# Expert blocks run in pairs, with rows turned two blocks ahead, and one dt product over 32 columns

## What is computed

```python
def expert_block(args):
    xb, e = args
    hb = jax.nn.silu(xb @ w_gate[e]) * (xb @ w_up[e])     # 2048 -> 512
    return hb @ w_down[e]                                 # 512 -> 2048
...
dt = jax.nn.softplus(dt_raw + dt_bias)      # dt_raw = the last 16 columns of h @ w_in
```

## Time and profile before

| | us |
|---|---|
| median of 3 runs | 2782.51 (2777.09 to 2786.82) |
| the profiled execution's own time | 2786.49 |
| its span, first to last instruction | 2784.8 |
| mean granted TensorE clock | 0.96 |

### The profile page before, as it was taken

How to read it: one execution, slowest core, us unless ns; L and a number is a source line. 1 busy time by engine, 2 the same in 40 slices (tenths; PEclk the granted TensorE clock), 3 DMA queues, 4 the chain that set the end, 5 groups by cost and what they waited for, 6 DMA issues and landing times.

```text
span 2784.8 us, 30586 instructions
## 1 busy us (share of the span) xinstructions
PE 2555.2 (92%) x11884; PEld 1529.8 (55%) x11884; DVE 1304.6 (47%) x1520; ACT 604.5 (22%) x859; POOL 296.9 (11%) x498
## 2 busy tenths in 40 slices
PE   4999999999999787899999499999999898999894
PEld 3577888888768666678887233333333333333331
DVE  4379999999766667544324411211122111111114
ACT  4122222222212365332344100000000000000003
POOL 0000000000111011010000011111111111111112
PEclk8999999999999879999999699999999999999997
DMA  9833333333676632655543999999949999799986
GB/s 337 314 115 99 98 106 98 98 109 107 215 225 202 223 122 87 253 171 155 199 161 131 401 408 417 353 401 407 410 143 383 410 408 362 278 415 401 413 325 254
DMA packets 233453, 710.94 MB, mean 255 GB/s; under 512 B 26266, under 2 KB 120618, under 8 KB 184790
## 3 DMA queue, kind: packets, MB, share of 16 engines
q1 hardware_dynamic: 186624, 555.56, 51.8%
q0 software_dynamic: 36736, 123.18, 14.4%
q10 hardware_dynamic: 9996, 30.86, 2.9%
HBM read 657.60 MB, written 70.86 MB: 262 GB/s over the span
## 4 chain that ended last, share of the span: by engine, by line
PE 37%; DMA 19%; DVE 2%; issue 0%; ACT 0%; POOL 0%; SPq 0%; ACTq 0%; DVEq 0%; POOLq 0%
PE ps L1696 15%; DMA ring<-in_w_up_dram 9%; DMA ring<-in_w_down_dram 9%; PE ps L1710 7%; PE ps L1916 4%; PE ps L1918 4%; PE ps L1917 4%; PE ps L1719 1%; PE ps L1636 1%; DVE tmp L2162 0%; PE ps L1931 0%; PE ps L1728 0%; DMA xrow<-h_d,tix 0%; DVE hidT L2455 0%; PE ps L1661 0%
## 5 line engine op out<-in xcount | busy, mean ns | idle before, releaser
L1696 PE MATMUL ps<-ring,xT 128*64 128x512 f32 x3136 | 702.2, 605 | 40.9 <-DMA ring<-in_w_up_dram 39.5
L1696 PEld LDWEIGHTS ps<-ring,xT 128*64 128x64 f32 x3136 | 232.5, 140 | 502.6 <-issue 499.0
L1710 PE MATMUL ps<-ring,hidT 128*64 128x512 f32 x1568 | 348.6, 596 | 10.8 <-DVE hidT L2455 6.0
L744 PE MATMUL ps<-hh,wih 128*128 128x512 f32 x1056 | 330.6, 394 | 7.4 <-DVE wil L732 7.4
L2450 DVE TENSOR_TENSOR hb<-ps,gsl 128x256 f32<-128x256 f32 x49 | 20.8, 424 | 673.5 <-ACT gsl L2125 673.5
L744 PE MATMUL ps<-hh,wil 128*128 128x512 f32 x1056 | 330.8, 394 | 0.0
L744 PE MATMUL ps<-hl,wih 128*128 128x512 f32 x1056 | 329.7, 393 | 0.0
L1115 DVE SCALAR_TENSOR_TENSOR acc<-u,vcur,acc 128x1024 f32<-128x1024 f32 x240 | 308.2, 1284 | 7.8
L2125 ACT ACTIVATE gsl<-ps 128x256 f32<-128x256 f32 x49 | 18.8, 383 | 1080.9 <-PE ps L1696 1080.9
L744 PEld LDWEIGHTS ps<-hh,wih 128*128 128x128 f32 x1056 | 198.7, 189 | 55.6 <-DVE wil L732 8.2
L1710 PEld LDWEIGHTS ps<-ring,hidT 128*64 128x64 f32 x1568 | 107.7, 137 | 217.9 <-issue 190.9
(11 more groups left out here) (387 smaller groups left out, 2907.8 us busy)
## 6 DMA issues: line engine op xcount, KB each, us to landing
ring<-in_w_gate_dram SPq DMA_DIRECT2D x128, 1024.0 KB, 30.1
ring<-in_w_up_dram SPq DMA_DIRECT2D x128, 1024.0 KB, 31.9
ring<-in_w_down_dram SPq DMA_DIRECT2D x64, 2048.0 KB
wm<-in_w_mod_dram POOLq DMA_DIRECT2D x88, 512.0 KB, 4.2
wraw_i<-in_w_in_dram SPq DMA_DIRECT2D x72, 512.0 KB, 3.9
wraw_o<-in_w_out_dram SPq DMA_DIRECT2D x128, 256.0 KB, 3.3
wmA<-in_w_mod_dram SPq DMA_DIRECT2D x32, 512.0 KB, 8.2
u<-in_w_mod_dram POOLq DMA_DIRECT2D x24, 512.0 KB, 4.6
```

What stands on the lines that cost most here:

```text
L744: last = pe.matmul(ps[:, 1024 * r + 512 * h:1024 * r + 512 * h + 512], w[:, s, k, :], x_[:, t, 512 * h:512 * h + 512], start=(t == 0 and n ...
L1696: last = pe.matmul(ps[BLK * a:BLK * a + BLK, BANK_GU:BANK_GU + FE], xT[:, t, h, :], ring[:, s:s + 2, c0:c0 + FE // 2], start=(q + k == 0), ...
L1710: last = pe.matmul(ps[BLK * a:BLK * a + BLK, BANK_D + 512 * n:BANK_D + 512 * n + 512], hidT[:, t, h, :], ring[:, slot(o, 8 + d), c0:c0 + 512],
```

## The change

In the first 29 experts (`PHASED`) the blocks of an expert are taken in passes of at most two; with an odd count the first pass has one block. A pass runs `gate_up`, all eight row turns (now of the block after the next) and `transpose_hidden` for each of its blocks, and then `down` for each. TensorE, VectorE and GpSimd each run nested loops for this: over passes, and in each pass over blocks, twice. The bounds are computed in registers (`passes`, `pass_blocks`). The turned hidden rows are kept in `hidR`, and copied from there in four parts of 64 columns into `hidT`. `down` makes one half of the output columns with all four parts and then the other; slots are released in the second. The output rows are scaled in two halves. The rows' scaling and shift are done in four quarters of 256 columns, each once `gate_up` has read that quarter of `xT`, and ahead of the hidden product. Gathers run three blocks ahead of the first in a pass instead of two, and rows of block 1 are turned before the first `gate_up`. In a pass GpSimd issues all gathers and then all scatters. The last three experts keep one block at a time, with the new waits and halves. `dt_proj` has both rounded parts of the weights side by side (32 columns) and two products instead of three; the two halves of the result are summed by a matmul with `dfold`.

```diff
--- before.py
+++ after.py
-NI = MAX_ITEMS + 3
+NI = MAX_ITEMS + 4
+AHEAD = 2
+PHASED = E - 3
...
-                                for n, (w, x_) in enumerate(((wdh, hh), (wdl, hh), (wdh, hl))):
-                                    last = pe.matmul(ps[0:H, 3072 + 512 * h:3584 + 512 * h], w[:, t, :],
+                                for n, x_ in enumerate((hh, hl)):
+                                    last = pe.matmul(ps[0:2 * H, 3072 + 512 * h:3584 + 512 * h], wd[:, t, :],
                                                      x_[:, t, 512 * h:512 * h + 512], start=(t == 0 and n == 0),
-                                                     stop=(t == KT - 1 and n == 2))
+                                                     stop=(t == KT - 1 and n == 1))
...
-                            last = pe.transpose(ps[:, 3584 + j * H:3584 + (j + 1) * H], sq[0:H, j * P:(j + 1) * P], ident[0:H, 0:H])
+                            last = pe.matmul(ps[:, 3584 + j * H:3584 + (j + 1) * H], sq[0:2 * H, j * P:(j + 1) * P], dfold[0:2 * H, :],
+                                             start=True, stop=True)
...
+            def passes(eng, begin, end):
+                count = eng.snap(nc.s_assert_within(end - begin, 1, SEQ // BLK, skip_runtime_bounds_check_because=COUNTED))
+                n = nc.s_assert_within(((count + 1) & 31) >> 1, 1, SEQ // BLK // AHEAD, skip_runtime_bounds_check_because=COUNTED)
+                head = nc.s_assert_within(((count - 1) & (AHEAD - 1)) + 1, 1, AHEAD, skip_runtime_bounds_check_because=COUNTED)
+                return eng.snap(n), eng.snap(head)
+            def pass_blocks(eng, begin, head, p):
+                later = (p + 7) >> 3
+                j0 = begin + (((p + 7) & 7) * AHEAD + head) * later
+                j1 = begin + head + p * AHEAD
+                return tuple(eng.snap(nc.s_assert_within(v, lo, MAX_ITEMS - 1 + lo, skip_runtime_bounds_check_because=COUNTED))
+                             for lo, v in enumerate((j0, j1)))
...
+                    pe.wait_ge(s_hb, j + 1)
                     for q in range(4):
-                        if q % 2 == 0:
-                            pe.wait_ge(s_xT, 2 * j + q // 2 + 1)
+                        pe.wait_ge(s_xT, 4 * j + q + 1)
                         for kind in (GATE, UP):
                             pe.wait_ge(s_we[2 * q + kind], 16 * o + 16)
                         s = slot(o, 2 * q)
                                                  ring[:, s:s + 2, c0:c0 + FE // 2], start=(q + k == 0), stop=(q + k == 6))
                         last.then_inc(s_guq[q], 1)
-                def down(pe, j, o):
-                    for d in range(FT):
-                        h, t = d // 2, d % 2
-                        if h == 0:
-                            pe.wait_ge(s_hT, 2 * j + t + 1)
-                        if t == 0:
-                            pe.wait_ge(s_we[8 + d], 16 * o + 16)
-                        for n in range(2):
+                def down(pe, j, o, turned):
+                    for n in range(2):
+                        pe.wait_ge(s_or, 2 * j + n + 1)
+                        for d in range(FT):
+                            h, t = d // 2, d % 2
+                            if n == 0:
+                                pe.wait_ge(s_hT, 4 * (j + turned) + d + 2)
+                                if t == 0:
+                                    pe.wait_ge(s_we[8 + d], 16 * o + 16)
                             for a in range(2):
                                 c0 = HALF_ROW * a + 512 * n
                                 last = pe.matmul(ps[BLK * a:BLK * a + BLK, BANK_D + 512 * n:BANK_D + 512 * n + 512],
                                                  hidT[:, t, h, :], ring[:, slot(o, 8 + d), c0:c0 + 512],
                                                  start=(d == 0), stop=(d == FT - 1))
-                        last.then_inc(s_dt[d], 1)
-
-                def transpose_rows(pe, ts):
+                            if n == 1:
+                                last.then_inc(s_dt[d], 1)
+                            elif d == FT - 1:
+                                last.then_inc(s_dn, 1)
+                def transpose_rows(pe, j, ts):
                     v = xrow[:].rearrange("p (c t) -> p t c", t=KT // 2)
                     for t in ts:
+                        if t == 0:
+                            pe.wait_ge(s_xr2, 16 * j + 16)
+                        if t % 4 == 0 and not (isinstance(j, int) and j == 0):
+                            pe.wait_ge(s_xm, 4 * j - 2 + t // 2)
                         last = pe.transpose(ps[:, BANK_X + t * P:BANK_X + (t + 1) * P], v[:, t, :], ident[:])
                         if t % 4 == 3:
                             last.then_inc(s_xt2, 1)
                 def transpose_hidden(pe, j):
-                    pe.wait_ge(s_hb, j + 1)
+                    pe.wait_ge(s_hb, j + 2)
                     v = hb[:].rearrange("p (c t) -> p t c", t=2)
                     for t in range(2):
-                        pe.transpose(ps[:, BANK_H + 512 * t:BANK_H + 512 * t + P], v[:, t, :], ident[:]).then_inc(s_hbt, 1)
+                        last = pe.transpose(ps[:, BANK_H + t * P:BANK_H + (t + 1) * P], v[:, t, :], ident[:])
+                    last.then_inc(s_hbt, 1)
...
-                        pool.wait_ge(s_xt2, 2 * i + 4)
-                        gather(i + 2, gix[:, ds(i + 2, 1)])
+                    words, begin = [packed_word(pool, 0)], 0
...
+                        with pool.Fori(0, count) as p:
+                            j0, j1 = pass_blocks(pool, begin, head, p)
+                            with pool.Fori(j0, j1) as i:
+                                pool.wait_ge(s_xt2, 2 * i + 6)
+                                gather(i + 3, gix[:, ds(i + 3, 1)])
+                            with pool.Fori(j0, j1) as i:
+                                scatter(i)
+                        begin = end
+                    with pool.Fori(begin, n) as i:
+                        pool.wait_ge(s_xt2, 2 * i + 6)
+                        gather(i + 3, gix[:, ds(i + 3, 1)])
                         scatter(i)
...
-                    transpose_rows(pe, range(8))
-                    begin = 0
+                    transpose_rows(pe, 0, range(8))
+                    transpose_rows(pe, 1, range(8))
+                    begin, turned = 0, 0
                     for o in range(E):
                         if o % PACK == PACK - 2 and o + 2 < E:
                             words.append(packed_word(pe, o // PACK + 1))
-                        end = blocks_through(words, o)
-                        with pe.Fori(0, end - begin) as b:
-                            j = begin + b
-                            gate_up(pe, j, o)
-                            pe.wait_ge(s_xr2, 16 * j + 32)
-                            transpose_rows(pe, range(7))
-                            transpose_hidden(pe, j)
-                            transpose_rows(pe, range(7, 8))
-                            down(pe, j, o)
+                        end = through(pe, words, o)
+                        if o < PHASED:
+                            n, head = passes(pe, begin, end)
+                            with pe.Fori(0, n) as p:
+                                j0, j1 = pass_blocks(pe, begin, head, p)
+                                done = pe.snap(turned + p)
+                                with pe.Fori(j0, j1) as j:
+                                    gate_up(pe, j, o)
+                                    transpose_rows(pe, j + 2, range(8))
+                                    transpose_hidden(pe, j)
+                                with pe.Fori(j0, j1) as j:
+                                    down(pe, j, o, done)
+                            turned = pe.snap(nc.s_assert_within(turned + n, 1, MAX_ITEMS, skip_runtime_bounds_check_because=COUNTED))
+                        else:
+                            with pe.Fori(begin, end) as j:
+                                gate_up(pe, j, o)
+                                transpose_rows(pe, j + 2, range(7))
+                                transpose_hidden(pe, j)
+                                transpose_rows(pe, j + 2, range(7, 8))
+                                down(pe, j, o, turned)
                         begin = end
...
+                        for q in range(4):
+                            h, a = q % 2, q // 2
+                            v = xT[:, 4 * a:4 * a + 4, h, :]
                             dve.wait_ge(s_xt2, 2 * j + a + 1)
-                            dve.tensor_tensor(xT[:, 4 * a:4 * a + 4, :, :],
-                                              ps[:, BANK_X + 512 * a:BANK_X + 512 * a + 512].rearrange("p (t h r) -> p t h r", t=4, h=2),
-                                              mods(mod_scale, a), ALU.mult).then_inc(s_xm, 1)
-                        for a in range(2):
-                            dve.wait_ge(s_xm, 2 * j + a + 1)
-                            v = xT[:, 4 * a:4 * a + 4, :, :]
```

(72 more changed lines are left out.)

52 lines of the change are left out of this document (36 added, 16 removed).

## The result

The changed kernel takes 3166.26 us (median; 3163.39 to 3169.0) against 2782.96 us for the kernel before on the same chip: ratio 1.1375, 95% interval 1.1356 to 1.1393. Forecast were 2796.5 us and a range of 2772 to 2832. The direction was right, the size was not: +383 us where +14 were expected. The profiled execution has a span of 3161.7 us (2784.8 before).

What follows compares the result with a forecast made beforehand. The prediction took TensorE's work and waits for weights, with clock lost behind them, as alternating limits in the expert stage. Stage +21.0 us, with dt +14.0, on a median of 2782.51 gave 2796.5 us, range 2772 to 2832.

Steps and rivals of the forecast that it cites:

- sequencers exposed: Rival: register arithmetic is not covered, 0.8 us a single pass, words 2.2, pairs 2; 2830 us, chance 0.15.
- Pass end: From gate/up's end to down: longer VectorE chain and copies start down at T + 3.2, +1.4 us each, 33 times.
- Between two gate/ups: Inside a pair, the loop jump and register instructions delay the next gate/up: +0.6 us, 10 times.
- VectorE behind a pair: The second block's output half waits for the first block's scatter, delaying VectorE's next work: +1.0 us, 10 times.
- Packed words: TensorE's load of a word loses the lead of queued down work that hid it: +1.2 us, 7 times.
- Start: Rows of block 1 must be gathered and turned before the first gate/up: +9.6 us, once.
- dt: In the dt products, 32 fewer matmuls save 7.4 us and eight folds cost 0.4: -7.0 us.
- The ring: Weight loads after a full ring issue 27.4 us before the expert ends, not 18.9; DMA runs 8.5 us further ahead.
- segments 1 and 2: Expert-stage blocks 23 to 34 and 35 to 45, each after a full ring; forecast -7.3 and -8.5 us.
- The ring wins: Rival: the longer chain at pass ends is hidden, so only the later start is paid; 2757 us, chance 0.14.
- Clock: Rival: about 1.6 us of TensorE idle at each pass end slows the next quarter; 2851 us, chance 0.06.
- Jumps: Rival: VectorE's nested loops make instructions be fetched again at pass ends, +55 us; 2838 us, chance 0.04.

Runs made afterwards that it cites:

- e6: The changed kernel with the growing sum worked out once a pass into a register, ahead of gate/up, except in the last three experts; 3074.47 us.
- e1: The changed kernel with the number of passes done kept in one TensorE register, one addition a pass, instead of the growing sum; 2804.88 us, ratio 1.0078.
- e5: The changed kernel with a pass-count register, hidden product ahead of the last quarter's scale and shift, hidden turns between row turns 0-3 and 4-7; 2796.22 us.
- e2: The kernel before with only the dt part of the change (two products over 32 columns and the fold); 2779.34 us, ratio 0.9988.
- e8: The changed kernel with a pass-count register, no hidR copy in the chain, part copies reading PSUM, order scale, product, shift; 2783.3 us, ratio 1.0003.
- e4: The kernel before, with blocks and order unchanged, plus the growing sum in an always-met wait ahead of down's matmuls; 3144.28 us, ratio 1.1301.
- e7: The changed kernel with a pass-count register, but down's first wait uses the growing sum except in the last three experts; 3084.4 us, ratio 1.1069.

## Why the prediction was wrong, and where it was right

**The step that failed** is the term "the pass arithmetic is some thirty instructions (about 3 us)", with "The arithmetic alone I cost at nothing, because the lead covers it just about". Three things in it were off. The number wasn't constant: ahead of a down it is 4 instructions in the first pass and 113 in a late one. The place wasn't the head of the pass but down's first wait, behind the hidden turn, where nothing is queued (a gap of 13.67 us for 14.0 us of arithmetic), and each down of a pair pays anew. And even at the head the cover is 3.5 us (e6). In place of nothing the sum cost 361 us (e1). The rate was well taken: 0.1 assumed, 0.12 measured. The rival *sequencers exposed* named this mechanism and gave it 0.15 and 2830: but its price was 0.8 us a single pass, where the late gaps are above 10. Of the 361 us, 304 are those gaps and 72 the matmuls that run slower behind them, less 15 us of waits for weights that vanished.

**Stage, without the sum.** e1 lets the other terms be read. From the first row turn to the end of the last down e1 takes 22.3 us more than the kernel before (1574.50 to 2770.1, against 1574.75 to 2748.1); the sum said +21.0. With dt the forecast was +14, and e1's ratio means +21.7 (14.2 to 29.5). But the parts balance by luck, for some were too dear and one too hopeful:

- *Pass end, +1.4 each.* Measured +1.32 (period 23.85 in e1); down starts 3.1 us after gate/up, forecast T + 3.2, and VectorE's part copy releases it, as said. e5 shows an error inside the chain: the product waits for ScalarE's silu until T + 0.5, and the scale ahead of it is free.
- *Between two gate/ups, +0.6.* +0.45 (16.05 in e1), 0.25 of it "issue".
- *VectorE behind a pair, +1.0.* Nothing. The scatter went as forecast: issued at D + 9.1, the second block's output half ran at D + 19.3, with D = 1669.65, down's start in e1 (below). But the halves, part copies and two quarters behind it end at D + 23.4, not D + 29, and TensorE's next gate/up ends at D + 27.7.

```profile
1669.65 13.95 PE L1740 MATMUL ps<-ring,hidT 128*64 128x512 f32 x64 [1.12 <-DVE hidT L2543]
1683.44 13.90 PE L1724 MATMUL ps<-ring,xT 128*64 128x512 f32 x64
...
1678.71 1.62 POOL L1898 DMA_INDIRECT x_d<-orow,oixc  x1 [0.34 <-issue]
...
1688.94 0.75 DVE L2556 SCALAR_TENSOR_TENSOR orow<-ps,gws,g2row 128x512 f32<-128x512 f32 x1 [11.19 <-DMA x_d<-orow,oixc]
...
1692.60 0.42 DVE L2521 TENSOR_TENSOR xT<-xT,mod_shift 128x256 f32<-128x256 f32 x1
```

- *Packed words, +1.2.* Close to nothing: in e1 two downs start 0.4 us later than the others, at 2175 and 2223 us.
- *Start, +9.6.* +9.8: first row turn to first gate/up is 1587.66 - 1574.50 = 13.16, against 3.40.
- *Last three experts, +0.5 a block.* Periods of 23.03 instead of 22.53: right.
- *dt, -7.0.* The products are 7.2 us shorter and the end is 3.3 (e2): the upper bound of 0, "if a later load's order takes it back", was nearer than I allowed.
- *The ring.* In e1 the first load behind the full ring is issued 27.1 us before the expert ends (forecast 27.4, 18.9 in the earlier trace rows):

```profile
2106.74 0.33 SPq L1527 DMA_DIRECT2D ring<-in_w_down_dram  x1
...
2133.82 13.90 PE L1724 MATMUL ps<-ring,xT 128*64 128x512 f32 x64
```

Yet segments 1 and 2 won 1.8 and 1.6 us, not 7.3 and 8.5 (block starts in e1: 2133.82, 2429.41, 2700.86). The 8.5 us that DMA runs ahead are an upper limit, and I took the limit for the value. By the measured terms the new pass ends, pairs and (in segment 2) unpaired blocks cost 13 and 11 us in these segments, so what the waits gave back, with the clock behind them, is 15 and 13 us of the 27.1 and 25.2; the sum let nearly all of it vanish. Segment 0 made up for it: +14.4 behind the start where 26.2 were forecast, by the terms that measured nothing. Why the waits of segments 1 and 2 went down by no more isn't settled; 8.5 and 8.5 us are still there, of 18.6 and 16.9 before.

**What I said would prove me wrong.** "Single periods stay below 23": no, they were 23.86. Weight waits that don't fall by half: they did (42.8 before with down's share, 18.1 in e1, at most 6 in the changed kernel, where DMA had all the time it wanted). Both tests passed and the forecast was still out by 370 us: neither looked at whether the period stays what it is in the first expert.

**The other rivals.** *The ring wins*: no, the pass end isn't hidden, e8 shows what it takes to hide it, and that 13 us come back. *Clock*: 1.1 us of idle behind each pass cost nothing (0.99 in e1); behind the gaps of 2.53 us and more in the changed kernel it did. *Jumps*: the instruction queue's packets went from 68 to 77 and to 70 in e1, still 0.2%, and e1 has all the nested loops with 2.3 us of "issue" before gate/up. The Trainium skill (Runtime: NRT & Kernel Launch, section Instruction fetch mechanics) lets a taken branch to a target outside the prefetched pages stall; no run here shows such a stall.

## What to carry to other kernels

A value that is named once in the code isn't held in a register for that reason: a running sum over a loop that is unrolled in the program grew with each turn here and was worked out again ahead of every down, so keep it in an allocated register that is added to. Ask of each register instruction where it stands: behind a wait for which the engine has nothing queued it cost its 0.12 us in full, under queued work only what exceeded 3.5 us. And look at a forecast's period late in the stage as well as in its first rounds.

## What the hardware showed beyond that

- At the end of a down TensorE's sequencer was 4.5 us ahead of the end of the last matmul: in e6 with a down of 13.95 us (2728.9 against 2733.37) and of 7.09 us (2765.2 against 2769.65), and in the kernel before (the loop's first instruction at 1599.1, down's end at 1603.58). At 13.95 us for 64 matmuls that makes some 20 matmuls, an estimate. The Trainium skill (Advanced Engine Details and Errata, section Engine Queue Depths) gives TensorE a queue of 64 and calls it complicated with tiling; here it is some 20 pairs of weight load and matmul, and the measurement decides.
- A register instruction of such a sum takes 0.12 us of the sequencer's time (14.0 us for 113), more than the 32 or 83 ns that its record shows.
- The clock behind a gap. Windows of the changed kernel in a late gap, in the down behind it and in the next gate/up (the clock stands ahead of the last two numbers):

```profile
2881.00:2892.70 11.70, 0.00 (x0) 0.00 (x0) 0.00 (x0) 0.00 (x0) 0.00 (x0) 0.56 1.01 416
2893.00:2900.00 7.00, 7.00 (x26) 2.23 (x26) 1.00 (x3) 0.00 (x0) 0.00 (x0) 0.77 0.14 43
2901.40:2915.00 13.60, 13.60 (x66) 4.72 (x62) 3.40 (x8) 0.00 (x0) 1.98 (x3) 1.00 0.73 297
```

In the gap the mean clock is 0.56, so nearly all of it is at the lower of its two levels (1.2 and 2.4 GHz, 0.5 and 1.00). In the seven us of the down behind it the mean is 0.77, between the two, and the next gate/up has the higher one throughout. So a gap costs the changed kernel's down 1.3 to 3.0 us once (8.4 to 10.1 for 7.09), whether it is 2.53 or 13.67 us long. Between 1.80 and 3.24 us the gap alone doesn't tell: 2.43 us cost 0.2 in the changed kernel (a pair's down, 14.16 for two), and 3.24 nothing in e6, while 1.80 in e4 made a down 8.78 us long, and 1.95 did so in e7, where the changed kernel's took 7.09 behind 1.95. The earlier trace rows has the same two faces at 2.49 and 2.68. What decides there isn't settled.
